# Three norm and weight-staging edits in a two-layer hybrid block kernel: down projection's weight slots, order of a tile's copies between two norms, an early square-root table

## The chip, the cores and the metric

The kernel runs on one core of one Trainium2 chip. A core has engines that run side by side, each with its own instruction stream, and that meet through semaphores: TensorE (matrix products, PE in the profile), VectorE (DVE), ScalarE (ACT), GpSimd (POOL), and the DMA queues, which SyncE (SP) fills. The metric is the time of the whole program on the device, in microseconds (us). Lower is better.

## What is computed

Everything is float32, for one sequence of 512 tokens and width 1024. Two layers of a first block are followed by one layer of a second block. Every linear layer is preceded by an RMS norm, and in the first block also followed by one.

```python
def rms_norm(x, gain):
    y = x * lax.rsqrt(jnp.mean(x * x, axis=-1, keepdims=True) + NORM_EPS)
    return y * gain

def swiglu(x, w_in, w_out):                    # w_in 1024 x 5632, w_out 2816 x 1024
    gate, up = jnp.split(x @ w_in, 2, axis=-1)
    return (jax.nn.silu(gate) * up) @ w_out

for l in range(2):                             # first block
    x = x + 0.5 * rms_norm(swiglu(rms_norm(x, ffn1_pre), w_ffn1_in, w_ffn1_out), ffn1_post)
    x = x + rms_norm(token_mixing(rms_norm(x, mix_pre), ...), mix_post)
    x = x + 0.5 * rms_norm(swiglu(rms_norm(x, ffn2_pre), w_ffn2_in, w_ffn2_out), ffn2_post)
    gate = jax.nn.sigmoid(rms_norm(x, ple_pre) @ w_ple_gate)
    x = x + rms_norm(gate * (p[l] @ w_ple_proj), ple_post)
# second block, once
x = x + concat(rms_norm(full_attention), rms_norm(dilated_attention)) @ w_out_2
x = x + conv_ffn(rms_norm(x), w_up, conv_w, conv_b, w_down)
```

`token_mixing` projects to 23 tiles of 128 columns, runs windowed attention, an mLSTM and an RWKV-7 recurrence on them, and projects back.

## The kernel before

**Products.** Each float32 operand is split into two parts, hi (rounded) and lo (the rest), and a product is three products: hi by hi, hi by lo, lo by hi. ScalarE writes the hi part with a copy and VectorE the lo part with a subtraction. This holds for weights (`w_space`, from `w_raw`: L186 and L193), for the normed input (`h_hi` L271, `h_lo` L303) and for the activations between the two halves of a feed-forward layer (L581, L596).

**Weight slots.** A unit is 128 x 1024 weights, 512 KB. SyncE loads units in a fixed order into four raw buffers (`load_to`, L172); a buffer is free when the lo part of the unit four places before has been written. The split parts go to one of 13 slots of `w_space`. Which slot a unit takes is written down in tables. Slots 0 to 10 also hold the activations of a feed-forward layer, two of its 22 rows in each; slots 11 and 12 are the `RING`. `hi_to` (L180) waits for the raw buffer and for the unit that last used the slot (`W.done`), in order of units.

**Stages.** An up projection (`Up`) goes through its units one at a time, `products_up` (L198) with 24 products over 512 tokens. Its first four units are done in two segments of 256 tokens (`tensor_first`, L323): a half tile is 24 products of 128x256. Segment 0 needs the normed tokens of tiles 0 and 1, segment 1 also those of tiles 2 and 3. A down projection (`Down`) goes through its 22 rows k (8 in the mixer's output): `tensor_row` (L365) does row k for all four token tiles, six products of 128x512 for each. The last four rows (`TAIL`) are done tile by tile instead (`tensor_tail`, L375), so that the output y of token tile 0 is ready three tiles before that of tile 3. The down rows used slots 11, 12, 11, 12, ... and 0 to 3 for the last four. The next layer's first six units (`EARLY`) take the slots of `FRESH`, `AFTER_OUT`, `AFTER_PLE` or `PLE_SLOTS`; ScalarE and VectorE split them before they start on the norms.

**Norms between layers.** `Turn` holds what leads from y of a token tile n to `h_hi` and `h_lo`. The post norm: ScalarE squares y with a running sum (L251) and takes a root (L253); VectorE multiplies y by the gain (L279), takes the reciprocal (L281) and updates x (L284). The pre norm: ScalarE squares x (L263) and takes a root (L265), VectorE takes the reciprocal (L290) and writes `h_tokens` (L296). TensorE then transposes `h_tokens` by eight products with the identity (L245; this is "the turn of tile n"), ScalarE copies the result to `h_hi` and VectorE subtracts to `h_lo`. `h_tokens` is one buffer. In the tail of a down projection the turn of tile 0 stands inside tile 2, and that of tile 1 inside tile 3; the turns of tiles 2 and 3 stand inside segment 0 of the next projection, behind the half tiles that `LATE_TURNS` names (`(0, 2): 3` is: behind segment 0, unit 2, turn tile 3). The order on ScalarE and VectorE is that of the two functions `turn_scalar` and `turn_vector` (L392, L405), for all junctions but two: `Ple` and the second block's output have their own. These functions serve ffn1 to mixer projection, mixer output to ffn2 and ffn2 to ple, in both layers, six times in all.

ScalarE evaluates Silu, Sigmoid, Sqrt and others by tables; when the next function isn't in the loaded one, an ACT_TABLE_LOAD stands ahead of it.

Of the kernel before, what the change touches and what calls it, by code (L numbers as in the profile page):

```python
# [10 lines left out]
ACT = mybir.ActivationFunctionType  # L11
# [3 lines left out]
P = 128  # L15
# [4 lines left out]
KF = FF // P  # L20
DEPTH = 2
DH = 64
NT = S // P
# [105 lines left out]
SPACE, RING = 11, (11, 12)  # L129
OPERANDS_AT = 7  # L130
UP = 2 * KF
TAIL = 4
EARLY = 6
FRESH = (4, 5, 6, 7) + RING
AFTER_OUT = (6,) + RING + (0, 1, 2)
AFTER_PLE = (9, 10, 4, 5, 6, 7)
OUT_SLOTS = RING + (0, 1, 2, 3, 4, 5)
PLE_SLOTS = (4, 5, 6, 7, 8) + RING + (0, 1, 2, 3)
PAIRS = ((0, 2), (2, 4))
IN_ORDER = (0, 1, 2, 3, 4, 5, 6, 7)  # L140
PLE_ORDER = (2, 3, 6, 7, 0, 1, 4, 5)
# [78 lines left out]
def pair(c, bank):  # L220
    return c.ps[:, bank:bank + 2, :].rearrange("p b n -> p (b n)")
# [126 lines left out]
class Down:  # L348
# [26 lines left out]
    def tensor_tail(self, pe, nc, operand, turn):  # L375
        c = self.c
        first = self.rows - TAIL
        for n in range(NT):
            for k in range(first, self.rows):
                if n == 0:  # L380
                    pe.wait_ge(c.W.lo_ready, self.d0 + k + 1)
                x_hi, x_lo = operand(k, n)
                m = products_down(nc, c, 2 * n, self.d0 + k, x_hi, x_lo, False, k == self.rows - 1)
                if n == NT - 1:
                    m.then_inc(c.W.done, 1)
                elif k == self.rows - 1:
                    m.then_inc(c.y_done, 1)
                if k == first + 1 and n >= 2:
                    turn.tensor(pe, nc, n - 2)


def turn_scalar(act, nc, turn, down, between=None):  # L392
    c = turn.c
    for n in range(NT):
        if n == NT - 1 and between is not None:
            between()
        down.wait_y(act, n)
        turn.scalar_post(act, nc, n, pair(c, 2 * n))
        turn.scalar_pre(act, nc, n)
        if n:  # L400
            turn.scalar_hi(act, nc, n - 1)
    turn.scalar_hi(act, nc, NT - 1)


def turn_vector(dve, nc, turn, between=None):  # L405
    c = turn.c
    for n in range(NT):
        if n == NT - 1 and between is not None:
            between()
        turn.vector_post(dve, nc, n, pair(c, 2 * n))  # L410
        turn.vector_pre(dve, nc, n)
        if n:
            turn.vector_lo(dve, nc, n - 1)
    turn.vector_lo(dve, nc, NT - 1)


LATE_TURNS = {(0, 0): 2, (0, 2): 3}


class Start:  # L420
# [97 lines left out]
            self.c.W.held[k // 2] = d0 + k  # L518


def down_slots():
    return tuple(RING[k % 2] for k in range(KF - TAIL)) + tuple(range(TAIL))


class Ffn(Up):

    def __init__(self, c, turn, w_in, w_out, slots, order=IN_ORDER, segments=PAIRS, before=None):
        super().__init__(c, turn, [w_in[n] for n in range(UP)], slots, order, segments, before)
        self.f0 = c.f_count
        c.f_count += KF  # L530
        self.a = Activations(c)
        d0 = len(c.W.units)
        self.a.release(d0)
        self.down = Down(c, [w_out[k] for k in range(KF)], down_slots())

    def wait_evacuated(self, pe, m):
        if m % 2 == 0:
# [2238 lines left out]
def first_block(nc, c, start, ffn, proj, following, consts):  # L2776

    with Stage(nc, c, "dense_start") as st:
        attention = WindowAttention(st, c, proj, 0, consts["window_masks"])
        factors = RwkvFactors(st, c, proj, attention, 0, consts["loras"], consts["reset"])  # L2780
        with nc.Block() as block:
# [19 lines left out]
            def _(pe):  # L2801
                start.tensor(pe, nc)
                ffn.tensor_first(pe, nc, LATE_TURNS)
                ffn.tensor_rest(pe, nc)
# [25 lines left out]
def middle_block(nc, c, name, mixout, ffn2, ple, ffn1, proj, following, table=None, layer=0, consts=None):  # L2830

    with Stage(nc, c, name) as st:
        after_ple = ffn1 or proj
# [3 lines left out]
        with nc.Block() as block:  # L2837
# [26 lines left out]
            @block.tensor  # L2864
            def _(pe):
                mixout.tensor(pe, nc)
                ffn2.tensor_first(pe, nc, LATE_TURNS)
                ffn2.tensor_rest(pe, nc)
                ffn2.tensor_down(pe, nc)
                ffn2.down.tensor_tail(pe, nc, ffn2.operand, ple.turn_in)  # L2870
                ple.tensor(pe, nc)
                after_ple.tensor_first(pe, nc, {(0, 1): 3})
                if ffn1 is not None:
                    ffn1.tensor_rest(pe, nc)
                    ffn1.tensor_down(pe, nc)
                    ffn1.down.tensor_tail(pe, nc, ffn1.operand, proj.turn)
                    proj.tensor_first(pe, nc, LATE_TURNS)
                    proj.tensor_with(pe, nc, attention, factors)
                else:
                    proj.tensor_rest(pe, nc)  # L2880
# [73 lines left out]
def place(nc, c, ctx):  # L2954

    def sb(name, shape, dt=F32):
        return ctx.enter_context(nc.sbuf_tensor(name, shape, dt))

    c.ps = ctx.enter_context(nc.psum_tensor("ps", [P, 8, S], F32))
    c.x = sb("x", [P, NT, D])
    c.mats = sb("mats", [P, len(MATS), P])
    c.mat = {m: c.mats[:, i, :] for i, m in enumerate(MATS)}
    c.vecs, c.vec2 = sb("vecs", [P, DEPTH, NVEC]), sb("vec_2", [P, NVEC2])
    c.eps, c.half_pi, c.freq = sb("eps", [P, 3]), sb("half_pi", [P, 1]), sb("freq", [P, 1])
    c.rope = sb("rope", [P, 2, S])
    c.sums, c.roots, c.inv = sb("sums", [P, 2, NT]), sb("roots", [P, 2, NT]), sb("inv", [P, 2, NT])
    c.group_root, c.group_inv = sb("group_root", [P, 2 * NT]), sb("group_inv", [P, 2 * NT])
    raw = sb("w_raw", [P, SLOTS, D])  # L2970
    base = -(-nc.sbuf_base // 64) * 64
    c.proj = sb("proj", [P, KEPT_TILES + 8, S])

    def at(name, shape, offset, dt=F32):
        return nc.alloc_sbuf_tensor_at(name, shape, dt, offset=base + offset)

    c.gpost, c.gpre = at("gain_post", [P, D], GAINS), at("gain_pre", [P, D], GAINS + 4096)
    c.space = at("w_space", [P, SPACE + 2, 2, D], SPACE_AT, F32R)
    c.h_hi, c.h_lo = at("h_hi", [P, KD, S], H_AT, F32R), at("h_lo", [P, KD, S], H_AT + 16384, F32R)
    c.squares = at("y_squares", [P, KD, S], H_AT)  # L2980
    c.gates = at("gates", [4, 2, S], H_AT + 28672)
    c.y = at("y", [P, KD, S], TEMPS)
    c.yg, c.hn = at("y_gained", [P, D], TEMPS), at("h_tokens", [P, D], TEMPS + 4096)
    c.pos_i = at("pos_i", [P, S], TEMPS, I32)
    c.s, c.p = at("act_s", [P, 2, S], TEMPS + 8192), at("act_p", [P, 2, S], TEMPS + 12288)
    c.conv = at("conv", [P, 4, S], TEMPS + 8192)
    c.junk = at("junk", [P, D], TEMPS + 16384, mybir.dt.bfloat16)
    c.s_wide, c.p_wide = (v[:, :, :].rearrange("p a n -> p (a n)") for v in (c.s, c.p))
    c.ang, c.turns, c.pos = c.p[:, 0, :], c.p[:, 1, :], c.s[:, 0, :]
    return raw  # L2990
# [24 lines left out]
def build(nc, a, out):  # L3015
# [3 lines left out]
    with ExitStack() as ctx:  # L3019
# [8 lines left out]
        for l in range(DEPTH):  # L3028
            ffn1.append(Ffn(c, turn, a["w_ffn1_in"][l], a["w_ffn1_out"][l], AFTER_PLE if l else FRESH, **after_ple))
            proj.append(MixProj(c, Turn(c, 4 * l + 1, 4 * l, True), a["w_in"][l], FRESH))  # L3030
            mixout.append(MixOut(c, Turn(c, 4 * l + 2, 4 * l + 1), a["w_out"][l]))
# [184 lines left out]
```

## Time and profile before

| | us |
|---|---|
| median of 3 runs | 3112.8 |
| lowest, highest run | 3106.61, 3112.91 |
| profiled execution | 3109.78 |
| its span | 3108.0 |
| PE busy | 2986.4 (96%) |
| DVE busy | 1387.9 (45%) |
| ACT busy | 1116.0 (36%) |
| mean granted TensorE clock | 0.97 |

A row of a timeline gives the start, the duration, the engine, the line, the operation with its tiles (out<-in) and shape, and a count. In brackets stands the idle time of the engine just before it and what ended it. The ends of TensorE's products are modelled, and neighbouring rows overlap by up to some 0.2 us. The granted clock is a share of full speed: 1.00 is 2.4 GHz, 0.50 is 1.2 GHz.

### The profile page before, as it was taken

The numbers are of one execution on the slowest core, as the hardware profiler recorded it, in microseconds if no ns is written. First come the engines' busy times: TensorE is split into PE (matmuls) and PEld (weight loads), VectorE is DVE, ScalarE is ACT, GpSimd is POOL, SyncE is SP. The second block draws the span as 40 slices with busy tenths as digits, with TensorE's granted clock in tenths as the row PEclk, the third lists the DMA queues.
The fourth block names the chain that finished last, engine by engine and source line by source line (L and its number), as shares of the span: only waits on it lengthen the run. The fifth ranks groups of instructions, "written<-read, shape, count | busy, mean of one in ns | idle before, by whom it ended". The sixth has DMA issues, their size and how long they took to land. (4 is left out here: it accounts for less than half of the span.)

```text
span 3108.0 us, 40759 instructions
## 1 busy us (share of the span) xinstructions
PE 2986.4 (96%) x17142; PEld 2516.0 (81%) x17142; DVE 1387.9 (45%) x1911; ACT 1116.0 (36%) x1576; POOL 12.8 (0%) x23
## 2 busy tenths in 40 slices
PE   8999999898999999999999898999999989999998
PEld 7888788777888878888888787888888878788887
DVE  3333445465333263333355464433254167556532
ACT  3222335334223153232334433322245255444431
POOL 0000000000000000000000000000000000000000
PEclk9999999898999999999999897999999989999999
DMA  4333311003233341333411103133332201213332
GB/s 146 99 95 114 128 46 56 24 2 102 76 101 109 95 149 42 101 95 114 142 33 62 32 2 102 48 95 97 114 122 88 82 13 36 72 65 96 101 95 81
DMA packets 71477, 254.40 MB, mean 82 GB/s; under 512 B 8056, under 2 KB 9208, under 8 KB 71296
## 3 DMA queue, kind: packets, MB, share of 16 engines
q1 hardware_dynamic: 71296, 251.81, 25.3%
q8 instruction: 136, 2.23, 0.3%
q14 instruction: 45, 0.37, 0.0%
HBM read 249.68 MB, written 2.10 MB: 81 GB/s over the span
## 5 line engine op out<-in xcount | busy, mean ns | idle before, releaser
L205 PE MATMUL ps<-h_hi,w_space 128*128 128x512 f32 (+1 forms) x5056 | 1451.0, 371 | 15.1 <-DVE h_lo L303 15.1
L205 PEld LDWEIGHTS ps<-h_hi,w_space 128*128 128x128 f32 x5056 | 924.6, 190 | 178.8 <-DVE h_lo L303 17.6
L193 DVE TENSOR_TENSOR w_space<-w_raw,w_space 128x1024 fp32r<-128x1024 f32 x440 | 535.9, 1224 | 1075.6 <-ACT w_space L186 1074.6
L205 PE MATMUL ps<-h_lo,w_space 128*128 128x512 f32 (+1 forms) x2528 | 933.3, 369 | 0.0
L186 ACT CAST w_space<-w_raw 128x1024 fp32r<-128x1024 f32 x440 | 457.7, 1047 | 986.2 <-PE ps L205 591.1
L215 PE MATMUL ps<-w_space 128*128 128x512 f32 x3312 | 766.3, 393 | 15.6 <-DVE w_space L193 14.8
L215 PEld LDWEIGHTS ps<-w_space 128*128 128x128 f32 x3312 | 625.3, 189 | 146.9 <-issue 11.3
L205 PEld LDWEIGHTS ps<-h_lo,w_space 128*128 128x128 f32 x2528 | 481.1, 190 | 78.5 <-issue 1.4
L581 ACT CAST w_space<-act_p 128x512 fp32r<-128x512 f32 x88 | 54.7, 621 | 189.3 <-DVE act_p L593 173.2
L596 DVE TENSOR_TENSOR w_space<-act_p,w_space 128x512 fp32r<-128x512 f32 x88 | 60.9, 692 | 70.7 <-ACT w_space L581 70.7
L593 DVE TENSOR_TENSOR act_p<-act_s,ps 128x512 f32<-128x512 f32 x88 | 59.8, 680 | 40.7 <-PE ps L205 40.7
L263 ACT ACTIVATE junk<-x 128x1024 bf16<-128x1024 f32 x40 | 42.3, 1057 | 92.2 <-DVE x L284 80.8
L245 PE MATMUL ps<-mats,h_tokens 128*128 128x128 f32 x320 | 46.0, 291 | 28.0 <-DVE h_tokens L296 28.0
L303 DVE TENSOR_TENSOR h_lo<-ps,h_hi 128x1024 fp32r<-128x1024 f32 x40 | 48.8, 1220 | 53.1 <-ACT h_hi L271 53.1
L215 PE MATMUL ps<-w_space,h_hi 128*128 128x512 f32 x256 | 69.2, 392 | 1.7 <-DVE h_lo L303 1.7
L245 PEld LDWEIGHTS ps<-mats,h_tokens 128*128 128x128 f32 x320 | 39.7, 150 | 33.6 <-DVE h_tokens L296 16.9
L2471 ACT ACTIVATE attn_probs<-ps 128x512 f32<-128x512 f32 x64 | 38.3, 598 | 71.4 <-PE ps L2381 71.1
L577 ACT ACTIVATE act_s<-ps 128x512 f32<-128x512 f32 x88 | 52.2, 594 | 24.4 <-PE ps L205 24.4
L271 ACT CAST h_hi<-ps 128x1024 fp32r<-128x1024 f32 x40 | 40.2, 1006 | 56.7 <-PE ps L245 56.6
L2391 PEld LDWEIGHTS ps<-v_tok,attn_probs 128*128 128x128 f32 x512 | 59.5, 192 | 1.3
L2391 PE MATMUL ps<-v_tok,attn_probs 128*128 128x65 f32 x512 | 58.8, 273 | 0.0
L296 DVE SCALAR_TENSOR_TENSOR h_tokens<-x,inv,gain_pre 128x1024 f32<-128x1024 f32 x40 | 51.4, 1285 | 13.9 <-PE ps L245 9.9
(379 smaller groups left out, 2412.2 us busy)
## 6 DMA issues: line engine op xcount, KB each, us to landing
w_raw<-in_w_ffn_in SPq DMA_DIRECT2D x176, 512.0 KB, 3.6
w_raw<-in_w_ffn_out SPq DMA_DIRECT2D x88, 512.0 KB, 3.5
w_raw<-in_w_in SPq DMA_DIRECT2D x64, 512.0 KB, 3.6
w_raw<-in_w_up SPq DMA_DIRECT2D x44, 512.0 KB, 3.5
w_raw<-in_w_out SPq DMA_DIRECT2D x24, 512.0 KB, 3.7
w_raw<-in_w_down SPq DMA_DIRECT2D x22, 512.0 KB, 3.5
w_raw<-in_w_ple_gate SPq DMA_DIRECT2D x16, 512.0 KB, 4.4
gain_pre<-in_gains_pre SPq DMA_DIRECT2D x10, 512.0 KB, 4.5
```

The costliest lines, as they stand in the source:

```text
L186: nc.scalar.copy(self.hi(n), self.raw[:, n % SLOTS, :]).then_inc(self.hi_ready, 1)
L193: nc.vector.tensor_tensor(self.lo(n), self.raw[:, n % SLOTS, :], self.hi(n).bitcast(F32), ALU.subtract).then_inc(self.lo_ready, 1)
L205: m = nc.tensor.matmul(c.ps[:, bank, t], part[:, cols], moving[:, k, t], start=(k == 0 and i == 0), stop=(k == KD - 1 and i == 2))
L215: m = nc.tensor.matmul(c.ps[:, bank + half, :], x, part[:, half * S:(half + 1) * S], start=(first and i == 0), stop=(final and i == 2))
L245: m = nc.tensor.transpose(c.ps[:, self.bank(n) + k // 4, (k % 4) * P:(k % 4 + 1) * P], c.hn[:, k * P:(k + 1) * P], c.mat["ident"])
L296: nc.vector.scalar_tensor_tensor(out=c.hn[:, :], in0=c.x[:, n, :], scalar=c.inv[:, 1, n:n + 1], in1=c.gpre[:, :], op0=ALU.mult, op1=ALU.mu ...
L303: nc.vector.tensor_tensor(c.h_lo[:, :, t], pair(c, self.bank(n)).rearrange("p (k m) -> p k m", k=KD), c.h_hi[:, :, t].bitcast(F32), ALU.su ...
L577: nc.scalar.activation(c.s[:, q % 2, :], c.ps[:, self.bank(n), :], ACT.Silu).then_inc(c.silu_ready, 1)
L581: nc.scalar.copy(self.a.hi(q), c.p[:, q % 2, :]).then_inc(c.act_hi, 1)
L593: nc.vector.tensor_tensor(c.p[:, q % 2, :], c.s[:, q % 2, :], c.ps[:, self.bank(n), :], ALU.mult).then_inc(c.product, 1)
L596: nc.vector.tensor_tensor(self.a.lo(q), c.p[:, q % 2, :], self.a.hi(q).bitcast(F32), ALU.subtract).then_inc(c.act_ready, 1)
L2391: m = nc.tensor.matmul(c.ps[:, 5 + h % 2, at:at + DH + 1], probs[:, h % 2, j, n * P:(n + 1) * P], c.v_tok[:, j, v, :], start=(j == 0), sto ...
```

## The change

The 22 rows of each feed-forward down projection take the slots of `DOWN_SLOTS`: the two ring slots at first, then also slots that its own activations held, once the second of their two rows is done. The tables of the next layer's early units follow. In `turn_scalar` and `turn_vector` the copies of tile n-1's h (for n = 1, 2) stand between the post and the pre norm of tile n, instead of behind the pre norm. The turns of tiles 0 and 1 in the tail come one row earlier. Ahead of the first post norm stands a one-column square root into `first_root`, and with it the table load where one is needed. The turn of tile 3 moves from behind unit 2 to behind unit 1 of segment 0, and after ple from unit 1 to unit 2.

```diff
+DOWN_SLOTS = (11, 12, 11, 12, 0, 11, 12, 1, 0, 11, 2, 12, 1, 3, 0, 11, 4, 2, 12, 5, 1, 3)
-FRESH = (4, 5, 6, 7) + RING
+FRESH = (6, 0, 11, 7, 4, 2)
-AFTER_PLE = (9, 10, 4, 5, 6, 7)
+AFTER_PLE = (9, 10, 6, 7, 4, 2)
-PLE_SLOTS = (4, 5, 6, 7, 8) + RING + (0, 1, 2, 3)
+PLE_SLOTS = (6, 0, 11, 7, 4, 2, 8, 12, 5, 1, 3)
...
-                if k == first + 1 and n >= 2:
+                if k == first and n >= 2:
                     turn.tensor(pe, nc, n - 2)
...
 def turn_scalar(act, nc, turn, down, between=None):
     c = turn.c
+    nc.scalar.activation(c.first_root[:, :], c.eps[:, 0:1], ACT.Sqrt)
     for n in range(NT):
         if n == NT - 1 and between is not None:
             between()
         down.wait_y(act, n)
         turn.scalar_post(act, nc, n, pair(c, 2 * n))
+        if 0 < n < NT - 1:
+            turn.scalar_hi(act, nc, n - 1)
         turn.scalar_pre(act, nc, n)
-        if n:
-            turn.scalar_hi(act, nc, n - 1)
+    turn.scalar_hi(act, nc, NT - 2)
     turn.scalar_hi(act, nc, NT - 1)
...
         turn.vector_post(dve, nc, n, pair(c, 2 * n))
+        if 0 < n < NT - 1:
+            turn.vector_lo(dve, nc, n - 1)
         turn.vector_pre(dve, nc, n)
-        if n:
-            turn.vector_lo(dve, nc, n - 1)
+    turn.vector_lo(dve, nc, NT - 2)
     turn.vector_lo(dve, nc, NT - 1)
...
-LATE_TURNS = {(0, 0): 2, (0, 2): 3}
+LATE_TURNS = {(0, 0): 2, (0, 1): 3}
...
-def down_slots():
-    return tuple(RING[k % 2] for k in range(KF - TAIL)) + tuple(range(TAIL))
...
-        self.down = Down(c, [w_out[k] for k in range(KF)], down_slots())
+        self.down = Down(c, [w_out[k] for k in range(KF)], DOWN_SLOTS)
...
                 ple.tensor(pe, nc)
-                after_ple.tensor_first(pe, nc, {(0, 1): 3})
+                after_ple.tensor_first(pe, nc, {(0, 2): 3})
```

What stands in a row on ScalarE, from the last weight copy of layer 0's ffn1 to the post norm of tile 2. Before:

```order
134 L186 CAST w_space<-w_raw 128x1024 [waits dense_mm_done,dense_w_raw_ready3]
135 L251 ACTIVATE junk,sums<-ps 128x1024 [waits dense_y_done]
136 L253 ACT_TABLE_LOAD
137 L253 ACTIVATE roots<-sums,eps 128x1 [waits dense_post_summed]
138 L263 ACTIVATE junk,sums<-x 128x1024 [waits dense_x_ready]
139 L265 ACTIVATE roots<-sums,eps 128x1 [waits dense_pre_summed]
140 L251 ACTIVATE junk,sums<-ps 128x1024 [waits dense_y_done]
141 L253 ACTIVATE roots<-sums,eps 128x1 [waits dense_post_summed]
142 L263 ACTIVATE junk,sums<-x 128x1024 [waits dense_x_ready]
143 L265 ACTIVATE roots<-sums,eps 128x1 [waits dense_pre_summed]
144 L271 CAST h_hi<-ps 128x8x128 [waits dense_turned]
145 L251 ACTIVATE junk,sums<-ps 128x1024 [waits dense_y_done]
```

In the changed kernel (its line numbers are one higher at these places):

```order
134 L187 CAST w_space<-w_raw 128x1024 [waits dense_mm_done,dense_w_raw_ready3]
135 L395 ACT_TABLE_LOAD
136 L395 ACTIVATE first_root<-eps 128x1
137 L252 ACTIVATE junk,sums<-ps 128x1024 [waits dense_y_done]
138 L254 ACTIVATE roots<-sums,eps 128x1 [waits dense_post_summed]
139 L264 ACTIVATE junk,sums<-x 128x1024 [waits dense_x_ready]
140 L266 ACTIVATE roots<-sums,eps 128x1 [waits dense_pre_summed]
141 L252 ACTIVATE junk,sums<-ps 128x1024 [waits dense_y_done]
142 L254 ACTIVATE roots<-sums,eps 128x1 [waits dense_post_summed]
143 L272 CAST h_hi<-ps 128x8x128 [waits dense_turned]
144 L264 ACTIVATE junk,sums<-x 128x1024 [waits dense_x_ready]
145 L266 ACTIVATE roots<-sums,eps 128x1 [waits dense_pre_summed]
```

The table load has moved ahead of the first square, which waits for y, and the copy of tile 0's h from behind to ahead of the pre norm of tile 1. VectorE's order moves in the same way.

What stands in a row on TensorE in the tail of the same down projection, up to the first product of the next. Before:

```order
1925 L215 MATMUL ps<-w_space 128x512 x41
1926 L245 MATMUL ps<-mats,h_tokens 128x128 [waits dense_hn]
1927 L245 MATMUL ps<-mats,h_tokens 128x128 x7
1928 L215 MATMUL ps<-w_space 128x512 x24
1929 L245 MATMUL ps<-mats,h_tokens 128x128 [waits dense_hn]
1930 L245 MATMUL ps<-mats,h_tokens 128x128 x7
1931 L215 MATMUL ps<-w_space 128x512 x12
1932 L205 MATMUL ps<-h_hi,w_space 128x256 [waits dense_w_lo_ready,dense_h_ready]
```

In the changed kernel:

```order
1925 L216 MATMUL ps<-w_space 128x512 x35
1926 L246 MATMUL ps<-mats,h_tokens 128x128 [waits dense_hn]
1927 L246 MATMUL ps<-mats,h_tokens 128x128 x7
1928 L216 MATMUL ps<-w_space 128x512 x24
1929 L246 MATMUL ps<-mats,h_tokens 128x128 [waits dense_hn]
1930 L246 MATMUL ps<-mats,h_tokens 128x128 x7
1931 L216 MATMUL ps<-w_space 128x512 x18
1932 L206 MATMUL ps<-h_hi,w_space 128x256 [waits dense_w_lo_ready,dense_h_ready]
```

Both turns of the tail stand six products earlier, and six more products stand between the turn of tile 1 and the next projection.

## Rows read from the trace of the kernel before

**Rows 1.** Waits of TensorE: engine, line, waited for: us in total, times, longest.

```profile
PE ps L245 <- DVE h_tokens L296: 28.0, 10, 10.8
PE ps L205 <- DVE h_lo L303: 15.1, 5, 3.5
```

**Rows 2.** Timeline of TensorE at the junctions: transposes and restarts; brackets: idle before.

```profile
376.04 1.09 PE L245 MATMUL ps<-mats,h_tokens 128*128 128x128 f32 x8 [1.02 <-DVE h_tokens L296]
...
389.68 0.58 PE L205 MATMUL ps<-h_hi,w_space 128*128 128x256 f32 x1 [3.45 <-DVE h_lo L303]
...
401.76 1.04 PE L245 MATMUL ps<-mats,h_tokens 128*128 128x128 f32 x8
...
752.87 1.03 PE L245 MATMUL ps<-mats,h_tokens 128*128 128x128 f32 x8
...
765.65 0.39 PE L205 MATMUL ps<-h_hi,w_space 128*128 128x256 f32 x1 [2.65 <-DVE h_lo L303]
...
775.24 1.03 PE L245 MATMUL ps<-mats,h_tokens 128*128 128x128 f32 x8
...
1120.61 1.09 PE L245 MATMUL ps<-mats,h_tokens 128*128 128x128 f32 x8 [0.80 <-DVE h_tokens L296]
...
1202.15 1.97 PE L245 MATMUL ps<-mats,h_tokens 128*128 128x128 f32 x8 [3.89 <-DVE h_tokens L296]
...
1554.30 1.10 PE L245 MATMUL ps<-mats,h_tokens 128*128 128x128 f32 x8 [2.15 <-DVE h_tokens L296]
...
1567.94 0.39 PE L205 MATMUL ps<-h_hi,w_space 128*128 128x256 f32 x1 [3.46 <-DVE h_lo L303]
...
1579.07 1.04 PE L245 MATMUL ps<-mats,h_tokens 128*128 128x128 f32 x8
```

**Rows 3.** Windows: stretch, length, busy us by engine, then granted clock, DMA share, GB/s.

```profile
570.00:763.00 193.00, 167.11 (x2101) 139.97 (x2100) 112.48 (x257) 77.49 (x136) 0.99 (x2) 0.89 0.13 44
1747.50:1953.40 205.90, 180.93 (x2100) 151.63 (x2098) 112.78 (x257) 77.36 (x136) 0.99 (x2) 0.82 0.13 41
1202.15:1208.00 5.85, 5.85 (x29) 5.85 (x30) 1.23 (x1) 2.30 (x2) 0.00 (x0) 0.53 0.01 3
```

**Rows 4.** Timeline of ScalarE, the first Silu after B and after D.

```profile
782.06 0.60 ACT L577 ACTIVATE act_s<-ps 128x512 f32<-128x512 f32 x1 [2.49 <-PE ps L205]
...
1214.41 0.60 ACT L577 ACTIVATE act_s<-ps 128x512 f32<-128x512 f32 x1 [7.94 <-PE ps L205]
```

**Rows 5.** Timeline of ScalarE and VectorE at B, layer 0.

```profile
744.91 1.02 ACT L251 ACTIVATE junk<-ps 128x1024 bf16<-128x1024 f32 x1 [4.34 <-PE ps L215]
...
750.66 1.28 DVE L296 SCALAR_TENSOR_TENSOR h_tokens<-x,inv,gain_pre 128x1024 f32<-128x1024 f32 x1
...
756.35 1.29 DVE L296 SCALAR_TENSOR_TENSOR h_tokens<-x,inv,gain_pre 128x1024 f32<-128x1024 f32 x1
...
760.08 1.28 DVE L284 SCALAR_TENSOR_TENSOR x<-y_gained,inv,x 128x1024 f32<-128x1024 f32 x1
...
762.78 0.99 ACT L271 CAST h_hi<-ps 128x1024 fp32r<-128x1024 f32 x1
...
764.38 1.22 DVE L303 TENSOR_TENSOR h_lo<-ps,h_hi 128x1024 fp32r<-128x1024 f32 x1
```

**Rows 6.** Timeline of ScalarE and VectorE at A, layer 0.

```profile
367.58 1.05 ACT L186 CAST w_space<-w_raw 128x1024 fp32r<-128x1024 f32 x1 [0.60 <-DMA w_raw<-in_w_in]
368.54 1.01 ACT L251 ACTIVATE junk<-ps 128x1024 bf16<-128x1024 f32 x1
369.66 1.28 ACT L253 ACT_TABLE_LOAD   x1
369.81 1.22 DVE L279 TENSOR_TENSOR y_gained<-ps,gain_post 128x1024 f32<-128x1024 f32 x1
370.95 0.29 ACT L253 ACTIVATE roots<-sums,eps 128x1 f32<-128x1 f32 x1
```

More of the change, by code:

```diff
@@ L2966, in place @@
     c.eps, c.half_pi, c.freq = sb("eps", [P, 3]), sb("half_pi", [P, 1]), sb("freq", [P, 1])
+    c.first_root = sb("first_root", [P, 1])
     c.rope = sb("rope", [P, 2, S])
```

## The prediction

> **What bounds the kernel now.** I read the list of waits of TensorE first. It is busy for 96% of the span, so a change can win only where TensorE stands still, or where its clock is low. By that list [rows 1] two waits belong to the places the diff touches: the transposes of L245 wait for `h_tokens` for 28.0 us in 10 waits, and the first products of an up projection (L205) wait for `h_lo` for 15.1 us in 5. Next I took the timeline of TensorE at each junction, where one linear layer ends and the norms lead into the next [rows 2]. I call them A (ffn1 to the mixer's projection, layer 0 at 376 us, layer 1 at 1554 us), B (mixer out to ffn2, 753 us and alike in layer 1), C (ffn2 to ple, 1121 us and alike in layer 1) and D (ple to the next up projection, 1202 us and alike in layer 1). The reader should see the idle time in brackets, and the distance between rows. From its restart to the transposes of tile 3, that is three half tiles and one turn, TensorE needs 775.24 - 765.65 = 9.59 us at B, but 401.76 - 389.68 = 12.08 us at A in layer 0 and 11.13 us in layer 1. The same work is slower after the longer stops (3.45 and 3.46 us, against 2.65 us at B). At D, after 3.89 us, the granted clock is 0.53 for the next 5.85 us [rows 3], mostly the lower of its two levels, 1.2 against 2.4 GHz. From the transposes to the first Silu, which waits for TensorE, it takes 1214.41 - 1202.15 = 12.26 us [rows 2, 4]; at B 782.06 - 775.24 = 6.82 us for one half tile less. A half tile is (9.59 - 0.85) / 3 = 2.91 us, with 0.85 us for a turn (1.03 us in its row, less the overlap with its neighbours, an estimate). So D loses 12.26 - 6.82 - 2.91 = 2.53 us to the clock.
>
> **The late restart of A and B (norm order, tail turns).** At B the copy of tile 1's h to `h_hi` starts at 762.78 us and `h_lo` ends at 765.60 us, when TensorE restarts [rows 2, 5]. Both stand behind the pre norm of tile 2 on their engines. In the new order they stand only behind the post norm of tile 2, whose update of x ends at 761.36 us [rows 5]; h_lo then needs 1.22 us more and ends near 762.7 us. The tail of TensorE ends no earlier than 763.0 us (765.65 less 2.65), so this wait goes. It cannot all be kept, since the turns move too. From the turn of tile 0 to the restart are 765.65 - 752.87 - 2.65 = 10.13 us of work, 36 products and two turns, so a product costs (10.13 - 1.7) / 36 = 0.234 us. The turn of tile 0 now comes six products earlier, 1.4 us, at 751.5 us; its h_tokens ends at 751.94 us [rows 5]. New wait: 0.5 us. Tile 1's turn is reached after 0.85 + 24 x 0.234 = 6.5 us, at 758.5 us, and has its h_tokens at 757.64 us [rows 5]: none. The restart comes at 752.0 + 1.4 + 10.13 = 763.5 us.
>
> **The turn of tile 3 one half tile earlier (A, B, the last block, the start).** It is reached 2 x 2.91 + 0.85 = 6.7 us after the restart, at 770.2 us. Its h_tokens takes from the square of the post norm to the end 751.94 - 744.91 = 7.03 us [rows 5], and the square starts some 0.2 us after the tail ends: 770.8 us. New wait 0.6 us, with nothing behind it that needed the turn so early. At the start and in the last block h_tokens of tile 3 is not in the tail's chain; I cost these two at nothing, between -0.6 and +0.6 us each. So A and B keep 1.1 us each. Bounds of that: nothing, if the chain is 0.6 us faster, and 2 us if each wait doubles.
>
> **The sum for A and B.** B loses now 2.65 us, at each layer: gain 2 x (2.65 - 1.1) = 3.1 us. A in layer 0 loses 1.02 + 0.16 us (the overlap of neighbouring rows that the wait also takes away) at the turn of tile 0, 3.45 at the restart, and 12.08 - 9.59 = 2.49 us by the clock, 7.1 us; in layer 1 2.15 + 0.16 + 3.46 + 1.54 = 7.3 us. Gain 6.0 + 6.2 = 12.2 us, if the square of tile 0 starts in time.
>
> **The new slots.** That is their part. At A the turn of tile 0 was due at 374.9 us; by the 7.96 us between square and turn at B the square could have started at 366.9 us. It started at 368.54 us, since ScalarE was still copying weights that came in by DMA (row at 367.58 us) [rows 6]. With only two ring slots the last rows and the six tiles of the next layer arrive in a bunch. Now row 4 of a down projection takes a slot that row 1 left, and later rows lead by up to eight rows; the last of the six early tiles waits for row 17 of 22, one tile's share of the tail (24 products, 5.6 us) before the square, and its two copies need 1.05 + 1.2 us. No row is ahead of fewer than three others except the first four, which stand as before.
>
> **The square-root table.** Its load takes 1.28 us and ends at 370.94 us, the root at 371.24 us; VectorE's multiply by the gain, which runs beside it, ends at 371.03 us [rows 6]. So the load delays the chain by 0.2 us only. Loaded ahead it lies in ScalarE's idle time after the last weight copy; B has no load at all there (its chain of 7.03 us shows what is left). I cost it at 0.2 us inside the above; it ranges from nothing to 1.6 us lost at each of the four junctions A and C, if the last copy is not early. The Trainium skill (ScalarE: Activation LUTs, "What ACT_TABLE_LOAD costs") states 2.66 us for a switch, with a drain. By that the load ahead would give 1.6 us a junction. The rows speak against it: the root starts 0.01 us after the load ends.
>
> **C and D.** C idles 0.80 + 0.16 us at the turn of tile 0 [rows 2], and keeps 0.5 us: gain 0.5 us, twice 1.0 us, layer 1 taken like layer 0. The rest of ple has its own order. At D the turn of tile 3 comes one half tile later. TensorE does 2.91 us of work in the 3.89 us and waits the last 1.1 us. The products that now go first use a bank whose values were read before h_tokens was formed, and h_lo of tile 3 is needed one half tile after the turn, 2.9 us, against 2.3 us for its two copies. With a stop of 1.1 us I expect no fall of the clock, since B's 2.65 us brought none. Gain 2.91 + 2.53 = 5.4 us, twice 10.9 us.
>
> **Sum.** 3.1 + 12.2 + 1.0 + 10.9 = 27.2 us. The profiled execution took 3109.8 us (span 3108.0), between the runs' lowest and their median of 3112.8 us; I predict 3109.8 - 27.2 = 3082.6, rounded to 3083 us.
>
> **Rivals.**
> 1. The clock still falls at both A and both D, by the shorter stops. The gaps close, but 2.49 + 1.54 + 2 x 2.53 = 9.1 us stay: 3092 us. For it: no row shows what two stops close together do. Against it: B. 8%.
> 2. The low-clock stretches elsewhere are drawn anew. The stage of the recurrence, which is not touched, took 193.0 us at a granted clock of 0.89 in layer 0, and 205.9 us at 0.82 in layer 1, with the same work [rows 3]. If both layers go one way, the time is 12.9 us more or less: 3070 or 3096 us. The Trainium skill (TensorE: Matmul & The Clock Gate, Part 1) says that the gate's watch runs free of the kernel's start, so that one kernel's count of slow matmuls varies from run to run. The two layers agree with that. 10%, half to each side.
> 3. The last copies are still late, since the DMAs and not the slots hold them. Then the square of tile 0 starts 1.6 us late, plus up to 1.6 us for the new root ahead of it, at four junctions, and the earlier turn waits for it: about 8 us of the gain go, 3091 us. 5%.
> 4. The copy of tile 0 waits for the turn and so holds back the pre norm of tile 1. It decides when the turn of tile 0 ends over 0.5 us late; then h_tokens 1 misses its turn and A keeps its restart: the gain is D and little more, 12 us or less, 3098 us. 4%, a quarter of it within 0.2%.
> 5. Slower. A row's slot is released too late, and TensorE waits for each row's copies. It decides where a row takes the slot of the row just before it: some 2.3 us (1.05 + 1.23) in each of 18 rows, in five down projections, 207 us, or 3290 us. The table names no such row. 2%.
>
> **How the numbers follow.** The forecast has 71%, and the rivals 29%. The range takes in 1, 2 and 3, and the runs' own spread of 6 us: 3067 to 3097 us. A measurement tells 0.2%, 6 us, from no change. Slower: 3% (rival 5, and a call that each early turn waits far longer than worked out); same 2%; faster 95%.
>
> **What would show it.** In the profile after, the L205 rows at A and B have no idle time before them; the turns of tiles 0 and 3 there wait 0.5 and 0.6 us; at D the wait is 1.1 us and the granted clock stays 1.00; the square of tile 0 at A starts as soon as TensorE's tile 0 is done, with the table load before it; and no L215 row in a down projection waits for w_space. I am wrong if a turn waits over 2 us, or if the clock falls at D.

## The result and the profile after

| | before | after |
|---|---|---|
| median of 5 runs, us | 3112.8 | 3086.89 |
| lowest, highest, us | 3106.31, 3117.71 | 3081.96, 3092.54 |
| profiled execution, its span, us | 3109.78, 3108.0 | 3081.96, 3080.2 |
| mean granted TensorE clock | 0.970 | 0.977 |

The ratio of the times is 0.9909, with a 95% interval from 0.988 to 0.9938: 26 us less in the medians, 27.8 us less between the two profiled spans. The forecast was 27.2 us less, or 3083 us.

The list of waits of TensorE after, beside [rows 1]; the lines of the code have moved on by one (engine, line, waited for: us in total, times, longest).

```profile
PE ps L246 <- DVE h_tokens L297: 21.2, 16, 11.1
PE ps L216 <- DVE w_space L194: 14.8, 3, 5.3
...
PE ps L206 <- DVE h_lo L304: 2.9, 1, 2.9
```

Of the five waits for `h_lo` one is left, at the program's start. The waits for `h_tokens` have become more and shorter, and 11.1 us of them are the start. The timeline of TensorE at the junctions shows where they stand (beside [rows 2]; brackets: idle before).

```profile
373.84 1.09 PE L246 MATMUL ps<-mats,h_tokens 128*128 128x128 f32 x8 [0.34 <-DVE h_tokens L297]
380.26 1.04 PE L246 MATMUL ps<-mats,h_tokens 128*128 128x128 f32 x8
381.06 4.33 PE L216 MATMUL ps<-w_space 128*128 128x512 f32 x18
385.23 0.28 PE L206 MATMUL ps<-h_hi,w_space 128*128 128x256 f32 x1
...
392.77 1.09 PE L246 MATMUL ps<-mats,h_tokens 128*128 128x128 f32 x8 [0.76 <-DVE h_tokens L297]
...
753.82 1.09 PE L246 MATMUL ps<-mats,h_tokens 128*128 128x128 f32 x8 [0.33 <-DVE h_tokens L297]
...
772.37 1.09 PE L246 MATMUL ps<-mats,h_tokens 128*128 128x128 f32 x8 [0.41 <-DVE h_tokens L297]
...
1118.84 1.09 PE L246 MATMUL ps<-mats,h_tokens 128*128 128x128 f32 x8 [0.32 <-DVE h_tokens L297]
...
1201.69 1.09 PE L246 MATMUL ps<-mats,h_tokens 128*128 128x128 f32 x8 [1.01 <-DVE h_tokens L297]
```

The reader sees at A (first four rows) that the next projection's first product at 385.23 us follows the tail without a bracket, where 3.45 us stood; that the turns of tiles 0 and 3 wait a little; and at D (last row) 1.01 us for 3.89. The granted clock behind D, over a window as long as the one in [rows 3], and over the stretch behind A's restart (stretch, length, busy us by engine, granted clock, DMA share, GB/s):

```profile
388.11:400.00 11.89, 11.13 (x95) 10.93 (x94) 5.09 (x5) 3.36 (x5) 0.00 (x0) 1.00 0.00 1
1201.69:1207.54 5.85, 5.85 (x50) 5.85 (x51) 1.22 (x1) 2.30 (x2) 0.00 (x0) 1.00 0.00 0
```

In 5.85 us TensorE does 50 products and transposes where it did 29. ScalarE at A in layer 0, beside [rows 6]:

```profile
361.35 1.05 ACT L187 CAST w_space<-w_raw 128x1024 fp32r<-128x1024 f32 x1 [4.39 <-PE ps L216]
362.42 1.28 ACT L395 ACT_TABLE_LOAD   x1
363.71 0.20 ACT L395 ACTIVATE first_root<-eps 128x1 f32<-128x1 f32 x1
366.74 1.02 ACT L252 ACTIVATE junk<-ps 128x1024 bf16<-128x1024 f32 x1 [2.82 <-PE ps L216]
```

The last weight copy ends 4.3 us ahead of the square, waits for TensorE and no longer for a DMA, and the table load lies in idle time.

**Where the 27.8 us are.** I cut both spans at six rows that both have: where TensorE starts the recurrence's transposes (L1517) and the mixer's output products in each layer, at the first head norm products (L2183), and at the second block's output products.

| stretch | before, us | after, us | moved | forecast |
|---|---|---|---|---|
| start to recurrence, layer 0 (A) | 578.49 | 572.32 | -6.2 | -6.0 |
| recurrence, layer 0 | 137.04 | 144.26 | +7.2 | 0 |
| output, layer 0, to recurrence, layer 1 (B, C, D, A) | 1040.22 | 1026.74 | -13.5 | -13.7 |
| recurrence, layer 1 | 149.42 | 142.67 | -6.7 | 0 |
| output, layer 1, to head norm (B, C, D) | 586.98 | 577.76 | -9.2 | -7.5 |
| head norm and attention | 193.72 | 194.43 | +0.7 | 0 |
| output to the end | 422.13 | 422.02 | -0.1 | 0 |

The three stretches that the change doesn't touch move by 7 us either way; in these two executions they cancel. The same windows of before and of after:

```profile
578.49:715.53 137.04, 118.44 (x1884) 100.17 (x1885) 79.53 (x216) 52.99 (x99) 0.00 (x0) 0.89 0.02 6
1755.75:1905.17 149.42, 131.68 (x1885) 111.47 (x1885) 79.85 (x216) 52.99 (x99) 0.00 (x0) 0.79 0.02 6
```

```profile
572.32:716.58 144.26, 126.37 (x1884) 105.75 (x1885) 80.08 (x216) 53.03 (x99) 0.00 (x0) 0.83 0.02 6
1743.32:1885.99 142.67, 123.83 (x1885) 104.77 (x1885) 79.80 (x216) 53.03 (x99) 0.00 (x0) 0.85 0.02 6
```

The counts of products are the same; the granted clock goes with the length. So for each kernel below I give, beside its ratio, its profiled span without these three stretches, the **rest**. Before it is 2627.8 us, after 2598.8 us: 29.0 us less. In second profiles of the two kernels it was 2627.4 and 2598.6 us, while their spans had moved by 2.5 and 1.2 us. So the rest is the finer measure, but it isn't free of chance: each is one profile, and with the old slots the waits of the turn of tile 0 at A and C sum to 5.30 and 5.42 us in the two profiles of before (1.02, 2.15, 0.80, 1.33 against 0.96, 0.27, 1.59, 2.60), and to 6.00 to 7.27 us in three kernels below that don't touch the chain of tile 0. A difference of 2 or 3 us in the rest is therefore read from rows, or not at all.

### The profile page after: what moved, and what is told of

Read it like the earlier page. It is cut to its first block and busy times, and to the rows that moved or that the text cites. A ratio compares the mean times of both kernels' runs of the same rounds, so it can differ in the third digit from the quotient of the medians.

```text
span 3080.2 us, 40766 instructions
## 1 busy us (share of the span) xinstructions
PE 2976.8 (97%) x17142; PEld 2505.0 (81%) x17142; DVE 1387.4 (45%) x1911; ACT 1118.0 (36%) x1582; POOL 12.8 (0%) x23
## 5 line engine op out<-in xcount | busy, mean ns | idle before, releaser
L206 PE MATMUL ps<-h_hi,w_space 128*128 128x512 f32 (+1 forms) x5056 | 1443.3, 369 | 2.9 <-DVE h_lo L304 2.9
L206 PEld LDWEIGHTS ps<-h_hi,w_space 128*128 128x128 f32 x5056 | 918.5, 189 | 164.9 <-DVE h_lo L304 3.7
L206 PE MATMUL ps<-h_lo,w_space 128*128 128x512 f32 (+1 forms) x2528 | 929.9, 368 | 0.0
L216 PE MATMUL ps<-w_space 128*128 128x512 f32 x3312 | 766.0, 392 | 15.6 <-DVE w_space L194 14.8
L216 PEld LDWEIGHTS ps<-w_space 128*128 128x128 f32 x3312 | 625.1, 189 | 146.8 <-issue 11.3
L206 PEld LDWEIGHTS ps<-h_lo,w_space 128*128 128x128 f32 x2528 | 477.4, 189 | 79.1 <-issue 1.4
L216 PE MATMUL ps<-w_space,h_hi 128*128 128x512 f32 x256 | 69.1, 392 | 1.7 <-DVE h_lo L304 1.7
L216 PEld LDWEIGHTS ps<-w_space,h_hi 128*128 128x128 f32 x256 | 47.6, 188 | 12.2 <-DVE h_lo L304 2.6
```

What stands on the lines that cost most here:

```text
L206: m = nc.tensor.matmul(c.ps[:, bank, t], part[:, cols], moving[:, k, t], start=(k == 0 and i == 0), stop=(k == KD - 1 and i == 2))
L216: m = nc.tensor.matmul(c.ps[:, bank + half, :], x, part[:, half * S:(half + 1) * S], start=(first and i == 0), stop=(final and i == 2))
```

## The experiments

**Each part alone, on the kernel before.** First the turn after ple:

```diff
-                after_ple.tensor_first(pe, nc, {(0, 1): 3})
+                after_ple.tensor_first(pe, nc, {(0, 2): 3})
```

> The kernel before, with one part of the change: after ple the turn of tile 3 stands behind unit 2 of segment 0 instead of unit 1. My theory: TensorE does a half tile (2.91 us) inside its stop of 3.89 us, waits the last 1.0 to 1.1 us, and its clock stays up, which gives 2.53 us more; 5.4 us at each of two places, 10.9 us less in all, ratio 0.9965. The rival that the clock falls in spite of the shorter stop: 5.8 us less, ratio 0.998, and a granted clock near 0.5 behind the turn.

Ratio 0.9982 (0.9958 to 1.0006); rest 2622.0 us, 5.8 us less. 5.8 us and 0.998 are the very numbers of the rival, that the clock falls all the same; the rows decide against it. At D itself it came as expected: waits of 0.98 and 1.02 us, and 6.88 us from the turn to the first Silu in layer 0, over which the granted clock was 1.00. But at C, which the edit doesn't touch, the turn of tile 0 waited 2.75 and 2.47 us, against 0.80 and 1.33 us in the first profile of before, and the clock fell behind both:

```profile
1134.04 1.97 PE L245 MATMUL ps<-mats,h_tokens 128*128 128x128 f32 x8 [2.75 <-DVE h_tokens L296]
```

```profile
1134.04:1140.00 5.96, 5.96 (x24) 5.19 (x25) 4.21 (x6) 2.93 (x5) 0.00 (x0) 0.73 0.01 3
```

C took back 3.1 us of waits and some 3 us of clock (an estimate from the granted clock of 0.73 and 0.72 over the 6 us behind each turn). That covers the distance from 10.9 to 5.8 us.

Second, the same stop filled with work that is of no use:

```diff
+                if (s, i) == again:
+                    products_up(nc, c, self.bank(i), self.u0 + i, a, b)
                 if (s, i) in turns:
                     self.turn.tensor(pe, nc, turns[s, i])
...
-                after_ple.tensor_first(pe, nc, {(0, 1): 3})
+                after_ple.tensor_first(pe, nc, {(0, 1): 3}, (0, 1))
```

> The kernel before, but ahead of the turn of tile 3 after ple TensorE does the 24 products of unit 1's half tile a second time, into the same bank (the same values again). No wait is removed: the turn still starts when h_tokens of tile 3 is there. My theory, that the slow stretch behind this turn is the clock's answer to 3.9 us without work: the stop shrinks to 1.0 us, the turn comes at the same distance from ple as before, and the stretch from the turn to the first Silu takes 9.7 us instead of 12.26; 2.5 us less at each of two places, 5.1 us in all, ratio 0.998, although 48 products are added. The rival, that something else slows the products there (contention, the semaphore's answer): no gain, 0 to 6 us more.

Ratio 1.0019 (1.0003 to 1.0035), a miss of the time; rest 2628.9 us, 1.1 us more. The rows at D are as expected:

```profile
1210.94 1.09 PE L245 MATMUL ps<-mats,h_tokens 128*128 128x128 f32 x8 [0.97 <-DVE h_tokens L296]
```

```profile
1210.94:1216.79 5.85, 5.85 (x50) 5.85 (x51) 1.22 (x1) 2.30 (x2) 0.00 (x0) 1.00 0.00 0
```

The clock stays at 1.00, and the first Silu comes 1220.71 - 1210.94 = 9.77 us after the turn, not 12.26. So the slow stretch of before was the clock's answer to the stop, and 2.5 us of each 5.4 at D are the clock's in that profile (1.5 us at layer 0 in the second profile of before, where the same stretch took 11.26 us). The time went elsewhere: at C the turn waited 2.94 and 2.68 us, with a fall behind each. Since no edit had touched C in either kernel, I profiled the kernel before once more (below). What part of the 1.0019 is C's and what part the recurrence's draw, the runs don't tell.

Third, the order of the norms:

```diff
+        if 0 < n < NT - 1:
+            turn.scalar_hi(act, nc, n - 1)
         turn.scalar_pre(act, nc, n)
-        if n:
-            turn.scalar_hi(act, nc, n - 1)
+    turn.scalar_hi(act, nc, NT - 2)
     turn.scalar_hi(act, nc, NT - 1)
...
```

(VectorE's lines in the same function are moved in the same way.)

> The kernel before, with the copies of h between the post and the pre norm for n = 1, 2, and nothing else of the change. My theory: the stop of 2.65 us at the restart of both B goes, with no new wait (the turns stand where they stood): 5.3 us. At A the square of tile 0 is still late and the turn of tile 0 still waits 1.0 and 2.1 us, but the restart waits no more than 0.5 us and its clock stays up: 3.0 + 2.5 us in layer 0, 3.0 + 1.5 us in layer 1. About 15 us in all, ratio 0.995. The rival, that the new order only makes the next step late (h_tokens of tile 2 or the post norm of tile 2): 5 us or less.

Ratio 0.9958 (0.9939 to 0.9976); rest 2612.6 us, 15.2 us less, as expected. No restart at A or B has idle time before it. It is the largest part that stands by itself. That the sum came out so near is in part chance: C's turn waited 2.59 and 1.55 us here, 2.0 us more than before, with a fall of the clock behind the first.

Fourth, the slots:

```diff
-FRESH = (4, 5, 6, 7) + RING
+FRESH = (6, 0, 11, 7, 4, 2)
...
-    return tuple(RING[k % 2] for k in range(KF - TAIL)) + tuple(range(TAIL))
+    return (11, 12, 11, 12, 0, 11, 12, 1, 0, 11, 2, 12, 1, 3, 0, 11, 4, 2, 12, 5, 1, 3)
```

(AFTER_PLE and PLE_SLOTS as in the change.)

> The kernel before, with the new tables of slots and nothing else of the change. My theory: the last weight copy on ScalarE is done some 3 us before the square of tile 0 can start, at A and C in both layers; the waits of the turn of tile 0 there (1.02, 2.15, 0.80, 1.33 us) go. The restart of A still waits as at B, 2.65 us, and by that shorter stop its clock stays up (2.5 and 1.5 us) and 0.8 us less is waited in each layer. 11 us in all, ratio 0.9965. The rival, that the DMAs hold the last copies and not the slots: waits as before, 0 us.

Ratio 0.9976 (0.996 to 0.9991); rest 2618.6 us, 9.2 us less where 11 were expected. The turn of tile 0 has no idle time before it at A or C, in either layer. The restart of A waits 3.05 us, 0.4 more than B, as much as the table load in its chain turns out to cost in the next experiment, and its clock still falls:

```profile
388.02 0.39 PE L205 MATMUL ps<-h_hi,w_space 128*128 128x256 f32 x1 [3.05 <-DVE h_lo L303]
```

**Each part taken away from the changed kernel.** Without the early root (its one line is removed):

> The changed kernel without the square root ahead of the first post norm, and so with the table load behind the first square again at A and C. My theory: the chain of tile 0 is 0.2 us longer there, four times 0.2 us, nothing that the times can tell: ratio to the kernel before like the changed kernel's. The rival after the skill's figure of 2.66 us for a switch: 1.4 to 1.6 us more at each of four places, 6 us, and the turn of tile 0 at A and C waits 1.8 us instead of 0.3.

Ratio 0.9874 (0.9848 to 0.9901); rest 2601.1 us, 2.3 us more than with it. The turn of tile 0 waits 0.75 us instead of 0.34 at A in layer 0, and 0.72 instead of 0.32 at the three other places with a load. The load costs 0.4 us of the chain, not 0.2, and not 1.5. The times don't show that gain: this kernel's median, 3078.07 us, is even the lowest of all, and its interval overlaps that of the changed kernel.

With the turn of tile 3 where it stood:

```diff
-LATE_TURNS = {(0, 0): 2, (0, 1): 3}
+LATE_TURNS = {(0, 0): 2, (0, 2): 3}
```

> The changed kernel with the turn of tile 3 behind unit 2 of segment 0 again, at the start, A, B and the last block. My theory: its wait (0.76 us at A in layer 0, 0.41 us at the other three) goes and nothing takes its place, 2.0 us less than the changed kernel, seen in the rows if not in the times. The rival, that the earlier turn relieves a later step (copies of units 4 and 5, the first Silu): a new wait at L206 or L577 and no gain.

Ratio 0.9894 (0.9867 to 0.9921); rest 2595.9 us, 2.9 us less than the changed kernel. The four waits are gone and no new one has come. With both kinds of turns back:

```diff
-                if k == first and n >= 2:
+                if k == first + 1 and n >= 2:
...
-LATE_TURNS = {(0, 0): 2, (0, 1): 3}
+LATE_TURNS = {(0, 0): 2, (0, 2): 3}
```

> The changed kernel with both kinds of turns back where they stood: tile 3 behind unit 2, and tiles 0 and 1 two rows into the tail instead of one. My theory: the turn of tile 0 waits no more (0.33 us at six places), the turn of tile 1 comes 1.1 us later than in the changed kernel, and h_lo of tile 1 ends near 0.3 us before the restart, since it then waits for the update of x of tile 2: no wait there. 4.0 us less than the changed kernel, ratio to the kernel before 0.9895. The rival: h_lo of tile 1 misses the restart by up to 1 us at four places, and the gain is lost again.

Ratio 0.9882 (0.9854 to 0.9909); rest 2592.0 us, 6.8 us less than the changed kernel. Without the new slots:

```diff
-DOWN_SLOTS = (11, 12, 11, 12, 0, 11, 12, 1, 0, 11, 2, 12, 1, 3, 0, 11, 4, 2, 12, 5, 1, 3)
+DOWN_SLOTS = tuple(RING[k % 2] for k in range(KF - TAIL)) + tuple(range(TAIL))
...
-FRESH = (6, 0, 11, 7, 4, 2)
+FRESH = (4, 5, 6, 7) + RING
```

(AFTER_PLE and PLE_SLOTS too.)

> The changed kernel with the old tables of slots. My theory: the last copies come late again, the square of tile 0 starts 1.6 us late at A in layer 0, 2.8 us in layer 1, 1.5 and 2.0 us at C, plus 1.3 to 1.6 us for the early root that now stands between the last copy and the square; the turn of tile 0 waits 2.5 to 5 us there. 12 us more than the changed kernel, more where the clock falls by it. The rival, that the slots do nothing: the same as the changed kernel.

Ratio 1.0000 (0.9983 to 1.0017); rest 2626.1 us. This is the surprise of the study: with all the other edits in place, the slots are worth the whole gain, 27.3 us of rest. Timeline of ScalarE and TensorE of this kernel at A:

```profile
368.21 1.05 ACT L187 CAST w_space<-w_raw 128x1024 fp32r<-128x1024 f32 x1 [0.93 <-DMA w_raw<-in_w_in]
369.28 1.28 ACT L395 ACT_TABLE_LOAD   x1
370.57 0.20 ACT L395 ACTIVATE first_root<-eps 128x1 f32<-128x1 f32 x1
370.68 1.00 ACT L252 ACTIVATE junk<-ps 128x1024 bf16<-128x1024 f32 x1
```

```profile
377.77 1.09 PE L246 MATMUL ps<-mats,h_tokens 128*128 128x128 f32 x8 [3.74 <-DVE h_tokens L297]
...
1135.21 1.97 PE L246 MATMUL ps<-mats,h_tokens 128*128 128x128 f32 x8 [4.68 <-DVE h_tokens L297]
...
1567.91 1.97 PE L246 MATMUL ps<-mats,h_tokens 128*128 128x128 f32 x8 [4.11 <-DVE h_tokens L297]
...
2324.06 1.97 PE L246 MATMUL ps<-mats,h_tokens 128*128 128x128 f32 x8 [5.18 <-DVE h_tokens L297]
```

The copies end late, the early root stands between them and the square, and the turn comes earlier to wait longer. The four waits sum to 17.7 us, against 1.3 us in the changed kernel; behind each the clock fell, to 0.73, 0.62, 0.58 and 0.70 over the next 6 to 7 us. That is some 9.4 us of clock (an estimate: the share missing from 1.00, times the stretch), and with the 16.4 us of waits it makes up 25.8 of the 27.3 us. In the last three rows the transposes themselves take 1.97 us instead of 1.09.

**A third set, on one chip.** The kernel before, unchanged:

> The kernel before, profiled once more, since kernels with the old slots showed waits of 0.8 to 2.9 us at the turn of tile 0 at C, and the stages that no kernel changes took 137 to 151 us from one profile to the next. My theory: the unchanged kernel does the same. Its two waits at C move by over 0.5 us from 0.80 and 1.33 us, and the stretch from the first transposes of the recurrence to the mixer's output differs by over 2 us from 137.0 us (layer 0) or 149.4 us (layer 1), while the stops at B (2.65 us) and D (3.89 us) come out within 0.1 us. The rival, that the edits caused these differences: all as in the first profile.

One time, 3112.29 us. At C the waits are 1.59 and 2.60 us, at A's turn in layer 1 it is 0.27 us where 2.15 stood; the recurrence takes 136.98 and 142.99 us, and head norm and attention 203.13 us where they took 193.72. B's stops are 2.65 us and 2.67, D's 3.85. So the waits behind DMA-bound copies move by themselves, and so do the stretches outside: of the two recurrences only layer 1's moved this time (149.42 us before), layer 0's came out as it was.

The changed kernel, and the one with both kinds of turns put back:

> The changed kernel again, timed beside the next one on one chip. Theory: ratio near 0.991; the turn of tile 0 waits 0.33 us at A, B and C, that of tile 3 0.4 to 0.8 us at A and B, D waits 1.0 us, as in its first profile, and the recurrence differs from 144.3 and 142.7 us. Without the three stretches that nothing changes, its span is 29 us under that of the kernel before.

> The changed kernel with both kinds of turns back where they stood before (tile 3 behind unit 2; tiles 0 and 1 two rows into the tail), again. Theory: the ten waits of the changed kernel at these turns are gone, 3.9 us in all, ratio to the changed kernel 0.9987 and to the kernel before 0.9895 to 0.988. Rival: its lead of 6 us in medians was the clock's draw, and beside the changed kernel it is within 1 us.

Changed: ratio 0.9895 (0.9867 to 0.9924), median 3081.99 us, rest 2598.6 us. Turns put back: 0.9881 (0.9853 to 0.9909), median 3080.26 us, rest 2591.5 us. The intervals overlap widely, so no time shows that the second is faster. Its rows do: at A,

```profile
374.22 1.04 PE L246 MATMUL ps<-mats,h_tokens 128*128 128x128 f32 x8
380.55 1.04 PE L246 MATMUL ps<-mats,h_tokens 128*128 128x128 f32 x8
381.34 3.01 PE L216 MATMUL ps<-w_space 128*128 128x512 f32 x12
384.19 0.28 PE L206 MATMUL ps<-h_hi,w_space 128*128 128x256 f32 x1
```

no row has a bracket. h_lo of tile 1 ended at 383.90 us (382.67 + 1.23 on VectorE), 0.3 us ahead of the restart. The waits of the changed kernel at these places sum to 4.0 us; the rest falls by 6.8 us in the first pair of profiles and by 7.1 us in the second. Part of the other 3 us is that a wait costs more than its bracket, since the overlap with the row before it goes too: from the turn of tile 3 at B to that of tile 0 at C this kernel takes 344.41 us and the changed one 346.47, 2.06 us less, where the moved turns (2.91 - 1.4) and the wait of 0.32 us make 1.83. At 0.2 us for each of ten waits that is an estimated 2 us. In the first pair some 1.4 us more lie between the output products of layer 0 and the turn at B, where the granted clock was 0.92 in the changed kernel and 0.96 with the turns back (0.95 and 0.96 in the second pair). What is left in the second pair, about 1 us, stays open.

Last, the old slots and no early root:

> The changed kernel with the old slots and without the early root: norm order and turns alone. Theory: with the last weight copies late, the early root stood between them and the square of tile 0; without it the turn of tile 0 waits about 1.1 us less at A and C (2.6 and 3.0 us instead of 3.74 and 4.11 at A, 3.6 and 4.1 instead of 4.68 and 5.18 at C), 4.4 us, and some of the clock's falls behind these stops go, 2 to 7 us more: ratio 0.997. The rival, that the root costs nothing there: ratio 1.0 as with it.

Ratio 0.9957 (0.9938 to 0.9977); rest 2616.9 us, 9.2 us less than with the root. The turn of tile 0 waits 2.54 and 1.98 us at A, and 4.52 and 3.99 us at C. The intervals of the two ratios, here and with the root, don't overlap. So the root is harmful where the copies are late: at A in layer 0 the square starts at 370.68 us with it and here at 369.03, 1.65 us earlier (0.13 of it since the last copy started earlier), and 0.4 is won back in the chain. It also says what the slots are worth without the root: 2616.9 - 2601.1 = 15.8 us, not 27.3.

| kernel | ratio to before | rest, us | less than before, us |
|---|---|---|---|
| ple turn alone | 0.9982 | 2622.0 | 5.8 |
| ple stop refilled | 1.0019 | 2628.9 | -1.1 |
| norm order alone | 0.9958 | 2612.6 | 15.2 |
| slots alone | 0.9976 | 2618.6 | 9.2 |
| all but the slots | 1.0000 | 2626.1 | 1.7 |
| all but slots and root | 0.9957 | 2616.9 | 10.9 |
| all but the root | 0.9874 | 2601.1 | 26.7 |
| all but the earlier turn 3 | 0.9894 | 2595.9 | 31.9 |
| all but the earlier turns 3, 0 and 1 | 0.9882, 0.9881 | 2592.0, 2591.5 | 35.8, 36.3 |
| the change | 0.9909, 0.9895 | 2598.8, 2598.6 | 29.0, 29.2 |

## Why the prediction was right, point by point

**Restart of A and B.** Right: no idle time is left before L206 at either, and the norm order alone does it. Its 15.2 us against 15 expected rest on the same working, with the chance named above. **Tail turns.** Forecast waits of 0.5 us; measured 0.32 to 0.34 us, six times. **Turn of tile 3.** Forecast 0.6 us; measured 0.76 us at A in layer 0, and 0.41 us three times. So A and B keep 0.73 to 1.1 us where the sum took 1.1. Nothing was won by the earlier turns, and they can be put back.

**D.** Right in both terms: the wait is 1.01 us (1.1 forecast), the clock stays up. The refilled stop shows the two terms apart, since it leaves the wait for `h_tokens` where it was and only gives TensorE work. The rival that the clock falls all the same has fallen.

**The slots.** The mechanism is right: the square of tile 0 starts when y is ready, and the rival that the DMAs alone hold the last copies has fallen, as the slots alone took away every wait of the turn of tile 0. The size was not forecast for itself but only as a condition of the sum. Rival 3 gave 8 us to their failing; taking them away cost 27 us of rest, 16.4 us of it in the four waits alone. The step that was mis-sized is the wait at C and A that late copies bring. I took layer 0's 0.80 us for both layers of C. With the old slots, and nothing changed in the chain of tile 0 at C, the same wait came out as 0.80, 1.33, 1.55, 1.59, 2.47, 2.59, 2.60, 2.68, 2.75 and 2.94 us (two each in before, twice, and in the ple turn, refilled stop and norm order alone), and behind the six from 2.47 us up the clock fell. Rival 3 left out the clock. The 6.2 us for A in layer 1 rest on such a draw too, a wait of 2.15 us that was 0.27 us in the second profile; that the four waits summed to nearly the same both times is luck.

**The root.** Forecast 0.2 us of the chain, from the end of the root against the end of the multiply. Measured 0.4. At A in layer 0 before, the square starts at 368.54 us [rows 6] and `h_tokens` ends at 375.98 us, just ahead of the transposes at 376.04 us [rows 2]: 7.44 us. At B it is 7.03 us [rows 5], and at A in layer 0 after it is 373.78 - 366.74 = 7.04 us. I had compared two ends, while without a load the row of the reciprocal starts before that of the multiply has ended (747.27 against 747.35 us at B). The Trainium skill's 2.66 us for a switch, load and drain together (ScalarE: Activation LUTs, "What ACT_TABLE_LOAD costs") is not what is seen here: loading earlier saved 0.4 us of the chain, the load's row is 1.28 us, and the root starts 0.01 us behind it.

**"B's 2.65 us brought no fall of the clock."** True of the two rows of that profile, and too weak a ground. Over the kernels with B's old restart (before twice, ple turn, refilled stop, slots alone) it stopped ten times for 2.64 to 2.67 us, and the clock fell behind three of them, as here in the slots-alone kernel:

```profile
765.83:772.00 6.17, 6.17 (x39) 6.17 (x40) 3.18 (x5) 2.03 (x4) 0.00 (x0) 0.72 0.01 3
```

That D stayed up was right, but by its 1.0 us: none of the stops of 1.6 us or less at A, B, C or D was followed by a fall in any profile, and each of the 17 stops of 3.45 to 3.90 us at A and D was. In between, the length alone doesn't decide: in the kernel without slots and root a stop of 1.98 us at A was followed by a fall (0.71 over the next 6 us) and one of 2.54 us was not (1.00).

**Rival 2** (the clock elsewhere is drawn anew) is what makes the spread: the recurrence took 137.0 to 150.6 us in layer 0 and 137.0 to 149.4 us in layer 1 over fourteen profiles. In the pair of the result it cancelled to 1.2 us, which is luck. **Rival 4** has fallen: `h_tokens` of tile 1 never made its turn wait, not even without the new slots, where the turn of tile 0 came 3.7 to 5.2 us late. **Rival 5** too: the wait of L216 for `w_space` is 14.8 us in 3 times as before, at the starts of the output products.

## What to carry to other kernels

What an edit is worth depends on what stands beside it: the new slots gave 9 us alone, 16 us beside all but the early root, and 27 us last, and the other edits without them gave nothing. For the early root it is shown that it makes a late copy cost more (9 us); for the earlier turns it is argued from the waits, as no run takes them back with the old slots. Take parts away from the finished change as well as adding them to the old kernel. Where a stop of 3.9 us shrank to 1.0 us here, more came back than the stop, since the clock stayed up; and where untouched stages draw their clock anew in each execution, compare the profiles stretch by stretch, leaving those stages out.

## What the runs showed that was not expected

- The same wait behind DMA-fed copies ranged over 2.1 us (0.80 to 2.94 us at C) in kernels that don't touch its chain, and moved by 0.8 and 1.3 us in the unchanged program, while waits bound by engines alone repeated to 0.05 us (B 2.64 to 2.67 us).
- A stop of 2.65 us is followed by a low clock in some executions and not in others (3 of 10), and a stop of 3.85 us at D by a short or a long one: 11.26 us from turn to Silu in the second profile of before, 12.26 us in the first.
- 5.8 us of useless products in two stops cost nothing where they stood: the turn's own wait shrank from 3.89 to 0.97 us, and what followed was faster.
